# A hybrid decoder step in five wide column blocks and two weight passes, conv taps read from PSUM, norms block by block

## The reference

```
h = rmsnorm(r, g_mix);  u | B | C | hv = h @ w_in              # 1024 -> 512 + 3*512
y_pool = pool_mix(u): trailing means over 2/4/8/16 tokens minus u, per group of 128
         channels, then @ w_pool[g] (128x128) * scale
y_conv = B * causal_dwconv3(C * hv)
r += concat(y_pool, y_conv) @ w_out                            # 1024 -> 1024
a | v = causal_dwconv3(rmsnorm(r, g_ffn) @ w_up)               # 1024 -> 2*2816
r += (silu(a) * v) @ w_down                                    # 2816 -> 1024
r += sigmoid(rmsnorm(r, g_ple) @ w_ple_gate) * (p @ w_ple_proj)   # p has width 256
y = rmsnorm(r, g_final)
```

## Time and profile before

| | |
|---|---|
| median of 3 runs | 965.77 us (964.0 to 978.27) |
| profiled execution, slowest core | 969.6 us (cores 956.0 to 969.6) |
| PE busy | 850.8 us, 5016 matmuls |
| DVE, ACT, POOL busy | 601.5, 466.4, 189.1 us |
| moved by DMA | 180.28 MB, mean 186 GB/s |

### The profile page before, as it was taken

The page is one execution under the profiler, slowest core; times in us unless marked ns, Lnnn a source line. Parts: engine busy times, 40 slices in busy tenths (PEclk is TensorE's granted clock), DMA queues, the critical chain, the costliest instruction groups (busy, mean ns, idle before and its releaser), DMA issues.

```text
span 969.6 us, 15050 instructions; the slowest of 8 cores (956.0 to 969.6 us)
## 1 busy us (share of the span) xinstructions
PE 850.8 (88%) x5016; PEld 831.8 (86%) x5016; DVE 601.5 (62%) x786; ACT 466.4 (48%) x627; POOL 189.1 (20%) x522
## 2 busy tenths in 40 slices
PE   2689899999987789989999998978879999999792
PEld 1588899999987688979999997868879999999792
DVE  0275588585842758459768582647647956767255
ACT  2122388184854523258547566332236724546632
POOL 4021023131300121013223220013102312222000
PEclk9999999999998999989999999979998888888996
DMA  9969648767753566997865775365895787588623
GB/s 241 299 154 255 179 115 233 199 193 208 191 167 88 139 173 173 267 293 204 228 188 166 215 218 169 92 160 131 210 285 144 178 209 174 143 226 197 168 52 116
DMA packets 90155, 180.28 MB, mean 186 GB/s; under 512 B 2656, under 2 KB 15712, under 8 KB 90080
## 3 DMA queue, kind: packets, MB, share of 16 engines
q0 software_dynamic: 81744, 159.67, 63.0%
q1 hardware_dynamic: 8336, 19.66, 7.2%
HBM read 169.87 MB, written 9.81 MB: 185 GB/s over the span
## 4 chain that ended last, share of the span: by engine, by line
PE 71%; DVE 13%; ACT 7%; issue 4%; DMA 2%; SPq 1%; DVEq 0%; POOL 0%; ACTq 0%; POOLq 0%
PE PS L282 51%; PE PS L296 18%; DVE SCR L304 6%; ACT SCR L301 4%; DVE R L304 3%; DMA SFs<-sf_in 2%; PE PS L410 2%; DVE SCR L307 2%; ACT GB L301 1%; DVE R L307 1%; ACT H L301 1%; DVE GB L307 1%; ACT DROW L301 1%; DVE GB L304 1%; SPq L315 1%
## 5 line engine op out<-in xcount | busy, mean ns | idle before, releaser
L282 PE MATMUL PS<-H,WS 128*128 128x344 f32 x2832 | 470.7, 329 | 9.7 <-DVE GB L304 4.0
L282 PEld LDWEIGHTS PS<-H,WS 128*128 128x128 f32 x2832 | 463.3, 197 | 14.1 <-issue 13.9
L307 DVE SCALAR_TENSOR_TENSOR SCR<-SCR,VEC 128x688 f32<-128x688 f32 (+1 forms) x288 | 266.2, 929 | 74.9 <-ACT SCR L301 55.9
L301 ACT ACTIVATE SCR<-PS 128x688 f32<-128x688 f32 x158 | 115.8, 737 | 182.4 <-PE PS L282 127.9
L301 ACT ACTIVATE SCR<-SCR,VEC 128x688 f32<-128x688 f32 x144 | 138.8, 964 | 76.7 <-DVE SCR L304 57.6
L282 PE MATMUL PS<-GB,WS 128*128 128x344 f32 x900 | 153.5, 327 | 5.0 <-DVE SFs L307 2.8
L282 PEld LDWEIGHTS PS<-GB,WS 128*128 128x128 f32 x900 | 147.3, 195 | 6.3 <-issue 6.3
L304 DVE TENSOR_TENSOR R<-PS,R 128x688 f32<-128x688 f32 x96 | 82.8, 872 | 93.6 <-PE PS L282 57.9
L296 PE MATMUL PS<-H,WS 128*128 128x344 f32 x432 | 87.4, 373 | 21.9 <-DVE H L307 15.8
L296 PEld LDWEIGHTS PS<-H,WS 128*128 128x128 f32 x432 | 85.1, 233 | 24.7 <-issue 24.7
L301 ACT ACTIVATE SCR<-SCR 128x688 f32<-128x688 f32 x102 | 79.2, 778 | 55.3 <-DVE SCR L304 33.8
(11 more groups left out here) (60 smaller groups left out, 391.5 us busy)
## 6 DMA issues: line engine op xcount, KB each, us to landing
WS<-w_up_u POOLq DMA_DIRECT2D x33, 2048.0 KB, 11.7
WS<-w_down POOLq DMA_DIRECT2D x12, 2048.0 KB, 11.4
WS<-w_in_c POOLq DMA_DIRECT2D x12, 1536.0 KB, 11.2
WS<-w_out POOLq DMA_DIRECT2D x6, 2048.0 KB, 11.1
WS<-w_gate POOLq DMA_DIRECT2D x6, 2048.0 KB, 11.1
WS<-w_down POOLq DMA_DIRECT2D x6, 1536.0 KB, 8.8
WS<-w_in_u POOLq DMA_DIRECT2D x3, 2048.0 KB, 11.2
R<-xT SPq DMA_DIRECT2D x2, 2752.0 KB, 27.8
```

Of the source, the lines that this page charges most:

```text
L282: ins = e.matmul(o, l, r_, start=st, stop=sp)
L301: P.op("act", (lambda e: e.activation(out=out, in_=in_, func=func, **kw)), r=r, w=w)
L307: P.op("dve", (lambda e: e.scalar_tensor_tensor(out=out, in0=in0, scalar=scalar, in1=in1, op0=op0, op1=op1)), r=r, w=w)
```

## The change

The columns are cut into five blocks of 416, 416, 416, 408 and 408 (`BW`, `BN`). Blocks 0 to 2 are the first pass over the weights, 3 and 4 the second, so weights are read twice. A matmul takes a whole block, with 16 halo columns for u, 2 for C, hv and the up projection: H keeps the blocks of a pass side by side behind a halo, so the product of the preceding tokens is computed again, and no halo is copied between rows. Elementwise instructions take a group `S` of one or two blocks. In the up projection all three taps are read from PSUM. Weights are packed on the host into 51 units of at most 1 MB, contiguous per partition, in a ring of five. The gate product of the up projection and the add to R in the gate stage are on POOL. Sigmoid becomes tanh with p halved. Norms are per block: while a block goes through w_out or w_down, the norm of the one before is finished and applied (`spread`); the gate stage has no product with the norm factor, as H is normalized first. In the first pass, units of w_out, w_down and the gate stay in the ring for all three blocks (`last`). States of the samples are folded by a few wide instructions. Inputs and outputs are stored per block, contiguous per partition.

```diff
-NT = 688
-NB = 344
-NSLOT = 3
-SLOTW = 4096
+BW = 416
+BN = (416, 416, 416, 408, 408)
+TILES = ((0, 1, 2), (3, 4))
+SUBS = (((0, 1), (2,)), ((3, 4),))
+NSCR = 8
+NW = 5
+WCOL = 2048
+NUNIT = 51
...
+        def mm(bank, S, lhs, rhs, rk, nk, wk, halo=0):
+            for bi, b in enumerate(S):
+                for k in range(nk):
+                    items.append((PS[:, bank + bi, 0:BN[b] + halo], lhs(k), rhs(b, k), k == 0, k == nk - 1))
...
+        def p_in(b):
+            P.dma("pool", "semPT", (lambda e: e.dma_start(out=PT[:, :, :], in_=pT[b])), w=["PT"])
+        def half_p():
+            act(PT[:, :, :], PT[:, :, :].bitcast(F32), AF.Copy, r=["PT"], w=["PT"], scale=0.5)
...
+        gate_first[0] = [rkey(0, 2)]
+        issue_units(limit=2)
+        x_in(1, 4, 0, 4, after=[("w", 0)])
...
+        def proj_block(b, units, nk, norm, hooks, kout=4, last=False):
...
+            mm_kouter(outs, rhs, rk, nk, [wkey(u) for u in units[0:(kout + 1) // 2]])
+            for oc in range(8):
+                if oc in bks:
+                    bk = bks[oc]
+                else:
...
+                    mm(bk, S, wlhs(u, nk, 256, oc % 2), rhs, rk, nk, [wkey(u)])
+                add_r(S, bk, oc)
+                norm.square(oc)
...
+                for f in hooks.get(oc, ()):
+                    f()
+                if last and oc % 2:
+                    done(units[oc // 2])
...
+        def spread(nm, gcol, first=1):
+            hk = {first: [nm.finish]}
+            for q in range(4):
+                hk[first + 1 + q] = [lambda k=k: apply_h(nm, gcol, k) for k in (2 * q, 2 * q + 1)]
+            return hk
...
+        def up(j, S, wi, post=()):
...
+            for q, c in ((0, j), (1, 22 + j)):
+                bk = banks(len(S))
+                mm(bk, S, wlhs(wi, 8, 256, q), lambda b, k: Hb(b, k, 2), lambda b, k: hrk(b, k, 2), 8,
+                   [wkey(wi)], halo=2)
+                A = next_scr()
...
+                act(scr(A, S), psv(bk, S, 2, n + 2), AF.Identity, r=pkeys(bk, S) + ["VEC"], w=[("scr", A)],
+                    scale=vcol(FW + 88 + c), bias=vcol(FB + c))
+                for d in (1, 2):
+                    stt(scr(A, S), psv(bk, S, 2 - d, n + 2 - d), vcol(FW + 44 * (2 - d) + c), scr(A, S),
+                        ALU.mult, ALU.add, r=pkeys(bk, S) + [("scr", A), "VEC"], w=[("scr", A)])
...
+            act(scr(a_, S), scr(a_, S), AF.Silu, r=[("scr", a_)], w=[("scr", a_)])
...
+            tt(Gs(S, jo), scr(a_, S), scr(v_, S), ALU.mult, r=[("scr", a_), ("scr", v_)],
+               w=[gkey(b, jo) for b in S], eng="pool")
...
+        def gate_block(b, gu, pu, hooks, last):
...
+            half_p()
+            nm = Norm(b, sq_G(b))
...
+            for oc in range(8):
+                bg = banks(1)
+                mm(bg, S, wlhs(gu[oc // 2], 8, 256, oc % 2), lambda b_, k: Hb(b_, k), lambda b_, k: hrk(b_, k),
+                   8, [wkey(gu[oc // 2])])
+                bp = banks(1)
+                mm(bp, S, lambda k: Wp[:, k, oc * 128:(oc + 1) * 128], lambda b_, k: PT[:, k, 0:n],
+                   lambda b_, k: ["PT"], 2, [wkey(pu)])
+                T = next_scr()
+                act(scr(T, S), psv(bg, S), AF.Tanh, r=pkeys(bg, S), w=[("scr", T)], scale=0.5)
+                stt(scr(T, S), scr(T, S), 1.0, psv(bp, S), ALU.add, ALU.mult,
+                    r=pkeys(bp, S) + [("scr", T)], w=[("scr", T)])
+                tt(Rb(b, oc), Rb(b, oc), SCR[:, T, 0, 16:16 + n], ALU.add, r=[rkey(b, oc), ("scr", T)],
+                   w=[rkey(b, oc)], eng="pool")
+                nm.square(oc)
+                if oc >= 3:
+                    nm.mm()
+                for f in hooks.get(oc, ()):
+                    f()
+                if last and oc % 2:
+                    done(gu[oc // 2])
+            if last:
+                done(pu)
...
+            for S in subs:
+                rows = [next_scr() for _ in range(4)]
+                for bi, b in enumerate(S):
+                    if t == 0 and b > 0:
+                        first_norm(b)
+                    if t == 1 and b == 4:
+                        nm = nrm["n1", 4]
+                        nm.finish()
+                        for k in range(8):
+                            apply_h(nm, GM, k)
+                    bk = [banks(1) for _ in range(4)]
+                    u_block(b, uu, bk)
+                    u_evac(b, bi, bk, rows)
+                tmp = [next_scr() for _ in range(4)]
+                for g in range(4):
+                    pool_chain(S, g, rows[g], tmp[2 * (g % 2)], tmp[2 * (g % 2) + 1])
```

More of the change, by code:

```diff
@@ new lines, in build_program, with banks, pkeys, hold_stat @@
+        rr = {"ps": 0, "scr": 0, "rs": 0}
+        held = set()
+        def banks(n):
+            p = rr["ps"]
+            while True:
+                if n == 2 and p % 2:
+                    p = (p + 1) % 8
+                if not any((p + i) in held for i in range(n)):
+                    rr["ps"] = (p + n) % 8
+                    return p
+                p = (p + 1) % 8
+        def pkeys(bank, S):
+            return [("ps", bank + i) for i in range(len(S))]
+        def hold_stat():
+            for c in (7, 6, 5, 4):
+                if c not in held:
+                    held.add(c)
+                    return c
+            raise AssertionError("stat banks")
@@ new lines, in build_program, with take, done, wlhs @@
+        unit_cols = [8] * 2 + [8] * 6 + [8] * 4
+        for pi, (j0, j1) in enumerate(PARTS):
+            unit_cols += [8] * (j1 - j0) + [j1 - j0] * 4
+        unit_cols += [8] * 5
+        assert len(unit_cols) == NUNIT
+        def take():
+            i = ust["next"]
+            ust["next"] += 1
+            assert i < ust["issued"], "unit not issued"
+            return i
+        def done(i):
+            ust["done"].add(i)
+            issue_units()
+        def wlhs(i, nk, ncol, c):
+            v = WS[:, i % NW, 0:nk * ncol].rearrange("p (k o) -> p k o", k=nk)
+            return lambda k: v[:, k, c * 128:(c + 1) * 128]
@@ new lines, in build_program, with first_norm, u_block @@
+        nrm = {}
+        def first_norm(b):
+            nm = Norm(b, sq_H(b), alt=True)
+            for k in range(8):
+                nm.square(k)
+                nm.mm()
+            nm.finish()
+            for k in range(8):
+                apply_h(nm, GM, k)
+        def u_block(b, uu, bk):
+            outs = [(bk[g], (b,), wlhs(uu[g // 2], 8, 256, g % 2)) for g in range(4)]
+            mm_kouter(outs, lambda b_, k: Hb(b_, k, 16), lambda b_, k: hrk(b_, k, 16), 8,
+                      [wkey(uu[0]), wkey(uu[1])], halo=16)
@@ L844, in build_program @@
+        assert ust["next"] == nunits
+        final_waits = [(s, P.count[s]) for s in sem_names
+                       if s in P.count and (s == "semO" or s.startswith("semY"))]
         with nc.Block() as block:
```

1241 lines of the change are left out of this document (570 added, 671 removed).

## The result

The changed kernel takes **1035.36 us**, the median of 4 runs (1032.81 to 1042.42). The kernel before, run beside it, takes 965.71 (4 runs). The ratio is 1.0698, 95% interval 1.0618 to 1.0778: 7% slower, outside my range of 912 to 1000. The profiled execution took 1035.31; its slowest core spans 1033.5 us. Views are of that core (5) where nothing else is said.

The account below looks back on a forecast made before the run. PE, busy 88%, was taken as the main bound, the gate being bound by a circle across engines. Stages summed to 932 us, plus 10 for 1.2 GHz and 18 for reduced clock: 960, or 956 against the median; range 912 to 1000.

Parts of the forecast that it names:

- 302 + 2 and 198 + 4: Feed-forward stages of first and second pass: matmul time plus waits, 304 and 202 us.
- under the next block: Feed-forward: block-by-block norms hide most of the old waits at part ends and norms beneath the following block's matmuls.
- let the first block start at 17: Start: 1.7 MB of x and 2 MB of weights at 253 GB/s allow block 0 to begin at 17 us.
- width alone gives 9: All matmuls: fewer, wider ones with the same 14.2 ns extra take 781 us against 790.
- the columns alone count: Rival, chance 0.20: 14.2 ns is part of a 157 ns floor, wide matmuls take 173 to 176 ns; total 912 us.
- 78.6 + 4.1 + 4: Second mixing part: 78.6 us, plus 4.1 for evacuation, Ln, Exp and first apply, plus 4; 87 us.
- some 16 us of waits a stage: Old feed-forward stage: 184.7 us held 169 us of matmuls, the rest being waits at part ends and norms.
- off 304 by over 15: Sign of being wrong: the three-block feed-forward stage differs from its forecast 304 us by more than 15.
- POOL add 1.0: Gate circle: POOL's add to R takes 1.0 us for 416 columns, within a round of 2.95 us.
- POOL takes 1.8: Rival, chance 0.12: POOL's gate add, under VectorE's products, takes 1.8 us instead of 1.0; 33 us more, total 989.
- The clock rival: Rival, chance 0.13: granted clock 0.81 holds in half the dense 700 us, total 987 us; in all, 1036.
- Waits I have not seen +20: Term of the forecast's own range of 935 to 985 us: unforeseen waits anywhere could add 20 us.

Follow-up runs that it names:

- the series: Changed kernel with 448 matmuls appended at its end, 64 in each of seven runs, 128 to 512 columns wide; 1108.7 us in one run.
- the best version: Changed kernel with late square, VectorE add, double-buffered p, earlier norms of blocks 2 and 4, four up projections first in both passes, statistics bank last; 945.4 us, ratio 0.970.

## Why the prediction was wrong

The mechanisms were mostly those I named. What failed is terms of the sum, nearly all to the same side. The first that failed is the feed-forward part, 302 + 2 and 198 + 4, where the waits were to hide "under the next block": it took 541 us for 506, for the last block of a pass has no next block. Then "let the first block start at 17", measured 27.7, in a first mixing part 27 us over. Then the second mixing part, whose 87 held no wait for VectorE's pool chain (7.6 us), 18 over. Then the gate, whose round and border price were right but not what PE waits for behind a border, 63 us lost for 44. My sum was 932 for the stages; measured, on the same cuts, by the windows above, they are 1033.5:

| stage | worked out | measured |
|---|---|---|
| mixing 1, with the start | 164 | 191.5 |
| feed-forward 1, with the wait for w_proj | 312 | 332.1 |
| gate 1, less that wait | 92 | 105.4 |
| mixing 2 | 87 | 104.9 |
| feed-forward 2, with its wait for w_proj | 210 | 226.1 |
| gate 2 and tail | 67 | 73.5 |

The 101 us between them, less 28 that I had set down for the clock, are the 73 that the forecast of 960 missed.

**Matmuls: near in price, wrong in form.** The turns were 188.1 to 188.8 at 416 columns for my 187.5, and 190.7 at 418 for 188.4: 3 to 10 us over 4180. That the extra stays the same with width failed: two rows at one width cannot tell an extra from a rate, and in the series it grows, 15.0 ns at 344 and 15.5 at 416. So "width alone gives 9" gave 4 at most, and the halo columns cost their 0.46 ns each. The rival "the columns alone count" is ruled out: nothing ran at 174 at full clock. (I priced it at 11.7 ns a matmul; my own rows gave 14.2, which would have been 53 us and 903.)

**Start and first mixing: 27 us short.** "Let the first block start at 17" took the bytes over a rate and left out the order: a quarter of x was queued behind weights, and 11 us were lost. "Partly at 1.2 GHz" was right in kind, half of each block, 9.0 and 9.2 us for my 8 and 7. The pool chain of VectorE was found and costed at 14.6 us; it ran from 54.1 to 70.9, 16.8 us, with PE waiting 15.4. Block 2 ended at 84.8 for 65. The run shows that it was worth only 9.5 to take the chain off this place. That another order of the first loads would win the 11 us back was not run.

**Second mixing: 18 us short.** My 78.6 + 4.1 + 4 held no pool chain, though I had costed the first pass's. It stands in the same place: VectorE has it from 651.9 to 669.0, and then PE's first conv product comes after 7.55 us of waiting (at 670.56, <-DVE SCR L173). The pool products wait 2.6 us more, and 13 of the first 32 matmuls ran at 1.2 GHz. No run took this wait away; the best version still has two waits of the kind, 7.4 and 6.1 us.

**Feed-forward: the gain at part ends came, and was given back at the pass's first up projection.** At the ends of parts PE hardly waits: 0.6 us in the first pass, 1.2 and 2.5 for POOL's gate product in the second, near my 4. But "some 16 us of waits a stage" had taken 169 us of matmuls for a stage; by the split above an old stage holds 8.4 to 10.3 us of waits, so there was less to win. And the first up projection, for which my sum held 2 us in the first pass and none in the second, waited 9.8 and 8.2: the last block of a pass has no next block to hide under. 306 us of matmuls (1608) ran in 322.9, so one of my signs of being wrong, off 304 by over 15, came. Four up projections ahead gave 10.2 of the first wait back.

**Gate: right mechanism, right round, short in sum.** I had put a loss of 44 us; it was 63. 2.95 was 3.01; 8 us for w_proj was 7.4 and then 5.1; the borders' 13 were 14 (for p's issue and landing I had put 0.7 + 3.3, the 3.3 from no row, and the trace has 3.7 for both); table loads after the border were counted, but not that PE then waits for a norm's Ln (10.8 us <-ACT RS). "POOL add 1.0" was 1.06 alone, but 1.20 on average, so rounds with norm products beside them took 3.25. That interference is the rival "POOL takes 1.8", at a small part of its size. Taking the add off POOL, or the square out of the circle, gave 35 and 39 us in the gates; the two overlap, for both together, with p loaded early, gave 65.

Of that rate the Trainium skill, page "GPSIMD Engine Reference", section "Performance versus the Vector engine", gave 0.91 us for 416 columns, an estimate in proportion; the trace has 1.06 alone. It states no price for VectorE beside it.

**The clock rival falls.** In the profiled execution no core stood at 0.81 at all, where cores of the old kernel's profile had up to 162 us of it. 1.2 GHz cost 33 us where 25 before; I had set 10 for it and 18 for 0.81, so that their sum of 28 came near was luck. On other chips 0.81 costs both kernels: core 0 of the run with the add on VectorE had 309 us at it and took 1021.6, core 4 none and 987.3, about 0.11 us lost for each us. The Trainium skill, page "TensorE: Matmul & The Clock Gate", "Part 1: The HAM clock gate", has this level as what sustained dense work on all cores gets; here cores of one run, under one kernel, had between 0 and 309 us of it, so what decides it stays open.

**The range.** "Waits I have not seen +20" is where the error sat. PE's waits rose by 69 us, 55 of them in the gates. What my stages had no room for is the start's order, the first up projection of each pass, the second pool chain, the waits for Ln behind a border and the interference in the gate, places of 5 to 20 us each.

## What to carry to other kernels

Where matmuls cost a rate per column, wider blocks buy nothing, so judge a re-tiling by its hand-overs alone: count the first and the last block of each pass, whose norm has nothing to hide under, and every operand that is loaded in place. In a circle over in-order engines, put the operation that closes it behind the next round's first one, before looking for a faster engine: that one line gave 39 us here. When a wait names one releaser, take it away in an experiment before believing its total: 34 us named p, and 14 were p's. And before work is moved to POOL, look at what VectorE reads beside it: with two operands in SBUF its taps took two to three times as long, with one in PSUM no longer.

## What the runs showed of the hardware that was not expected

- A back-to-back fp32r matmul with its weight load takes 0.454 to 0.462 ns a column at full clock from 256 to 512 columns, and 112 ns at 192 and at 128.
- A VectorE operation of 416 columns with both tensor operands in SBUF lasts 0.65 us alone, and 1.48 beside POOL's add, 1.93 on average beside POOL's products of the up projection; 816 columns take 1.07 and 2.42. With one operand in PSUM it lasts 0.64 beside POOL too. POOL's add takes 1.04 to 1.08 alone and 1.26 to 1.37 beside such an operation.
- The granted 0.81 does not go to a whole die: in the run with the add on VectorE it was 309 us on cores 0 and 1, some 150 on 2, 3, 6 and 7, none on 4 and 5.
